# Gate products of a gated recurrence on half the rows, both gates in one product

## What is computed

```
xg = conv.reshape(B, T, LRU_BLOCKS, LRU_BLOCK_W)          # 8 blocks of 64 channels
r = sigmoid(einsum('btnd,nde->btne', xg, w_r) + b_r)
i = sigmoid(einsum('btnd,nde->btne', xg, w_i) + b_i)
log_a = -LRU_C * r * softplus(-lam);  a = exp(log_a)
mult = where(pos == 0, 1, sqrt(-expm1(2 * log_a)))
u = mult * i * conv
h_t = a_t * h_(t-1) + u_t
```

## Time and profile before

| | us |
|---|---|
| median of 3 runs (701.61 to 701.86) | 701.74 |
| the profiled execution | 701.76 |
| its span, first to last instruction | 700.0 |
| TensorE busy | 692.3 (99%), 4688 products |
| VectorE busy | 303.2 (43%) |
| ScalarE busy | 263.0 (38%), 642 instructions |
| POOL busy | 106.1 (15%) |

### The profile page before, as it was taken

How to read it: one execution, slowest core, us unless ns; L and a number is a source line. 1 busy time by engine, 2 the same in 40 slices (tenths; PEclk the granted TensorE clock), 3 DMA queues, 4 the chain that set the end, 5 groups by cost and what they waited for, 6 DMA issues and landing times.

```text
span 700.0 us, 11867 instructions
## 1 busy us (share of the span) xinstructions
PE 692.3 (99%) x4688; PEld 671.7 (96%) x4688; DVE 303.2 (43%) x668; ACT 263.0 (38%) x642; POOL 106.1 (15%) x231
## 2 busy tenths in 40 slices
PE   8999999999999999999999999999999999999998
PEld 8999998999999999999999999899999999999998
DVE  6462452343434448875433374317533672500000
ACT  7562242322323343756616555325543460200000
POOL 0002171435354000000002222122100000000000
DMA  8402105122120311011041010131001351522221
GB/s 301 183 0 92 61 1 194 48 65 61 51 75 7 119 61 60 7 56 61 1 145 66 11 61 1 49 97 62 1 1 61 119 183 32 166 71 64 65 66 37
DMA packets 26803, 50.07 MB, mean 72 GB/s; under 512 B 2232, under 2 KB 20152, under 8 KB 24540
## 3 DMA queue, kind: packets, MB, share of 16 engines
q1 hardware_dynamic: 26748, 49.31, 21.4%
HBM read 42.22 MB, written 9.12 MB: 73 GB/s over the span
## 4 chain that ended last, share of the span: by engine, by line
PE 96%; DMA 1%; DVE 1%; issue 1%; ACT 1%; POOL 0%; SPq 0%; DVEq 0%; ACTq 0%
PE proj L409 22%; PE proj L411 22%; PE proj L410 22%; PE branch L411 4%; PE branch L410 4%; PE branch L409 4%; PE branch L589 2%; PE branch L654 2%; PE branch L631 2%; PE branch L505 1%; PE branch L522 1%; PE branch L537 1%; PE branch L543 1%; PE branch L644 1%; PE branch L525 1%; DMA mixed<-x_T 1%
## 5 line engine op out<-in xcount | busy, mean ns | idle before, releaser
L409 PE MATMUL proj<-big 128*128 128x352 f32 (+1 forms) x952 | 305.8, 321 | 1.6 <-DVE big L1148 1.2
L411 PE MATMUL proj<-big 128*128 128x352 f32 (+1 forms) x952 | 290.8, 305 | 0.0
L410 PE MATMUL proj<-big 128*128 128x352 f32 (+1 forms) x952 | 290.8, 305 | 0.0
L409 PEld LDWEIGHTS proj<-big 128*128 128x128 f32 x952 | 179.3, 188 | 5.4 <-ACT big L814 2.0
L410 PEld LDWEIGHTS proj<-big 128*128 128x128 f32 x952 | 179.4, 188 | 2.6 <-issue 1.9
L411 PEld LDWEIGHTS proj<-big 128*128 128x128 f32 x952 | 179.3, 188 | 0.0
L1143 DVE TENSOR_TENSOR big<-raw,big 128x512 fp32r<-128x512 f32 x72 | 48.8, 689 | 39.3 <-ACT big L808 39.3
L1588 POOL TENSOR_SCALAR stat<-stat 128x1 f32<-128x1 f32 (+2 forms) x68 | 18.0, 264 | 278.7 <-ACT junk L934 189.5
L411 PE MATMUL branch<-m_hi,big 128*128 128x352 f32 x180 | 58.0, 322 | 0.0
L410 PE MATMUL branch<-m_lo,big 128*128 128x352 f32 x180 | 58.0, 322 | 0.0
L409 PE MATMUL branch<-m_hi,big 128*128 128x352 f32 x180 | 57.9, 322 | 0.0
(11 more groups left out here) (219 smaller groups left out, 964.5 us busy)
## 6 DMA issues: line engine op xcount, KB each, us to landing
raw<-w_units SPq DMA_DIRECT2D x17, 1024.0 KB, 4.9
mixed<-x_T SPq DMA_DIRECT2D x12, 352.0 KB, 7.9
xy<-x_T SPq DMA_DIRECT2D x24, 176.0 KB, 2.4
out_y_T<-xy SPq DMA_DIRECT2D x24, 176.0 KB, 1.9
raw<-w_out SPq DMA_DIRECT2D x6, 512.0 KB, 4.5
xy<-w_out SPq DMA_DIRECT2D x6, 512.0 KB, 4.2
s<-state_ret SPq DMA_DIRECT2D x4, 512.0 KB, 3.9
out_s_ret<-s SPq DMA_DIRECT2D x4, 512.0 KB, 3.2
```

Source lines behind the costliest of these rows:

```text
L409: pe.matmul(out, a_lo, b_hi, start=first, stop=False)
L410: pe.matmul(out, a_hi, b_lo, start=False, stop=False)
L411: return pe.matmul(out, a_hi, b_hi, start=False, stop=last)
```

## The change

The gate weights are laid out anew: for stage h, the upper 64 partitions hold the r and the i block of the first 64 channels side by side (64 x 128), the lower 64 partitions the i and the r block of the other 64 channels. A product uses 64 partitions of weights and input and gives both gates of 64 channels. There are still 6 per stage, now two for each chunk (upper, lower) in banks 0 to 4 and 0. Each bank is read by two tangents of 64 partitions, so 12 per stage; one of the two moves its half to the other 64 partitions (in the upper product the second, in the lower the first), so all count in `gates_read` is doubled. The sixth product waits for 12f+2. The first tangent of a stage now waits for `lru_set` f (from f = 1 on) besides the product. On ScalarE the stage is split over three slots: tangents of the first two chunks at the old slot, the last chunk one slot later, the decay step two slots later; the slots of m2, root and scan move by two. The biases are laid out to match.

```
-            wg = sb("wg", [P, 2, H, P], scope=r)
+            wg = sb("wg", [P, H, P], scope=r)
...
-            ("conv", (90, 98, 108, 119)), ("gates", (95, 106, 117, 128)), ("m2", (100, 111, 122, 133)),
-            ("sqrt", (101, 112, 123, 134)), ("scan", (102, 113, 124, 135)))}
+            ("conv", (90, 98, 108, 119)), ("gates", (95, 106, 117, 128)), ("last", (96, 107, 118, 129)),
+            ("decay", (97, 108, 119, 130)), ("m2", (102, 113, 124, 135)), ("sqrt", (103, 114, 125, 136)),
+            ("scan", (104, 115, 126, 137)))}
...
-            GATE_BANKS = [0, 1, 2, 3, 4, 0]
...
-                for q in range(6):
-                    gate, c = divmod(q, 3)
-                    if q == 5:
-                        pe.wait_ge(S_["gates_read"], 6 * f + 1)
-                    elif f > 0:
-                        pe.wait_ge(S_["gates_read"], 6 * f)
-                    pe.matmul(bb[GATE_BANKS[q]][:, 0:CH], wg[:, gate, f, :], cv[:, f % 2, c * CH:(c + 1) * CH],
-                              start=True, stop=True).then_inc(S_["gates_done"], 1)
+                for c in range(3):
+                    for part in range(2):
+                        q, rows = 2 * c + part, slice(64 * part, 64 * part + 64)
+                        if q == 5:
+                            pe.wait_ge(S_["gates_read"], 12 * f + 2)
+                        elif f > 0:
+                            pe.wait_ge(S_["gates_read"], 12 * f)
+                        pe.matmul(bb[q % 5][:, 0:CH], wg[rows, f, :], cv[rows, f % 2, c * CH:(c + 1) * CH],
+                                  start=True, stop=True).then_inc(S_["gates_done"], 1)
...
-            def lru_sig(f):
...
+            def lru_sig(f, cs):
+                if f >= 1:
+                    act.wait_ge(S_["lru_set"], f)
+                if f == 0:
+                    act.wait_ge(S_["decay_set"], 1)
+                low, high = slice(0, 64), slice(64, P)
+                for c in cs:
+                    cols = slice(c * CH, (c + 1) * CH)
+                    for part in range(2):
+
+                        q = 2 * c + part
+                        act.wait_ge(S_["gates_done"], 6 * f + q + 1)
+                        bank, b = bb[q % 5], half_b[:, H * part + f:H * part + f + 1]
+                        first = rgs[low, f % 2, cols] if part == 0 else ig[high, cols]
+                        second = ig[low, cols] if part == 0 else rgs[high, f % 2, cols]
+                        act.activation(first, bank[low, 0:CH], ACT.Tanh, bias=b[low], scale=0.5).then_inc(
+                            S_["gates_read"], 1)
+                        act.activation(second, bank[high, 0:CH], ACT.Tanh, bias=b[high], scale=0.5).then_inc(
+                            S_["gates_read"], 1)
+
+            def lru_decay(f):
+                act.wait_ge(S_["gates_read"], 12 * f + 12)
...
                 if (u, s) in LRU_AT["gates"]:
-                    lru_sig(LRU_AT["gates"][u, s])
+                    lru_sig(LRU_AT["gates"][u, s], (0, 1))
+                if (u, s) in LRU_AT["last"]:
+                    lru_sig(LRU_AT["last"][u, s], (2,))
+                if (u, s) in LRU_AT["decay"]:
+                    lru_decay(LRU_AT["decay"][u, s])
...
-    wg = np.zeros((P, 2, H, P), np.float32)
...
+    wg = np.zeros((P, H, P), np.float32)
+    r_blocks, i_blocks = f["w_rgate"][0], f["w_igate"][0]
+    for h in range(H):
+        wg[:64, h] = np.concatenate([r_blocks[2 * h], i_blocks[2 * h]], axis=1)
+        wg[64:, h] = np.concatenate([i_blocks[2 * h + 1], r_blocks[2 * h + 1]], axis=1)
```

More of the change, by code:

```diff
@@ L316, in _ @@
             sp.wait_ge(S_["stored_ret"], 32 * H)
-            sp.dma_start(wg[:].rearrange("p a h n -> p (a h n)"), io["w_gates"]).then_inc(S_["wg_in"], 16)
+            sp.dma_start(wg[:].rearrange("p h n -> p (h n)"), io["w_gates"]).then_inc(S_["wg_in"], 16)
             for u in range(9, 13):
@@ L582, in lru_gates @@
                     pe.wait_ge(S_["mix_a"], 36)
[L583 to L590 removed]
+                for c in range(3):
[7 more added lines that the diff above has]
+                                  start=True, stop=True).then_inc(S_["gates_done"], 1)
             def turn_tails():
                 pe.wait_ge(S_["lru_set"], H)
[L594 removed]
+                pe.wait_ge(S_["gates_read"], 48)
                 for f in range(H):
@@ L608, in turn_k @@
                 else:
-                    pe.wait_ge(S_["gates_read"], 24)
+                    pe.wait_ge(S_["gates_read"], 48)
                 pe.transpose(bb[0][:, 0:n], kn[0:n, n9 % 2, :], ident[0:n, 0:n]).then_inc(S_["kT_done"], 1)
@@ L892, in ret_norm @@
                     act.activation(o_nrm[:, m % 2, 0:NS], bb[1 + m % 2][:, 0:NS], ACT.Copy).then_inc(S_["o_set"], 1)
-            def lru_sig(f):
[L895 to L906, removed]
-                                   ACT.Tanh, bias=half_b[:, col:col + 1], scale=0.5).then_inc(S_["gates_read"], 1)
-                act.wait_ge(S_["gates_read"], 6 * f + 6)
+            def lru_sig(f, cs):
[18 more added lines that the diff above has]
+                act.wait_ge(S_["gates_read"], 12 * f + 12)
                 if f > 0:
@@ L1720, in laid_out @@
     put("conv_b", f["conv_b"].reshape(H, P))
-    put("b_r", f["b_rgate"].reshape(H, P))
-    put("b_i", f["b_igate"].reshape(H, P))
+    b_r, b_i = f["b_rgate"].reshape(H, P), f["b_igate"].reshape(H, P)
+    put("b_r", np.concatenate([b_r[:, :64], b_i[:, :64]], axis=1))
+    put("b_i", np.concatenate([b_i[:, 64:], b_r[:, 64:]], axis=1))
     put("lam", f["lru_lambda"].reshape(H, P))
@@ L1728, in laid_out @@
             par[r, PAR["sink_s"] + half] = f["attn_sinks"][0, 2 * half + r // DS % 2]
-    wg = np.zeros((P, 2, H, P), np.float32)
-    for a, name in enumerate(("w_rgate", "w_igate")):
-        blocks = f[name][0]
-        for n in range(2 * H):
-            r = slice(64 * (n % 2), 64 * (n % 2) + 64)
-            wg[r, a, n // 2, r] = blocks[n]
+    wg = np.zeros((P, H, P), np.float32)
[3 more added lines that the diff above has]
+        wg[64:, h] = np.concatenate([i_blocks[2 * h + 1], r_blocks[2 * h + 1]], axis=1)
     x = np.concatenate([f["x_prompt"].reshape(SEQ, D), f["x_sample"].reshape(NS, D)])
@@ L1741, in laid_out @@
         "qk_gain": np.concatenate([f["q_norm_g"][0], f["k_norm_g"][0]]),
-        "w_gates": wg.reshape(P, 2 * H * P), "state_ret": f["state_ret"][0],
+        "w_gates": wg.reshape(P, H * P), "state_ret": f["state_ret"][0],
         "cache_k": f["cache_swa_k"][0],
```

## The result

The changed kernel took 711.93 us (median of 4 runs, 711.7 to 712.61) against 701.67 us before (4 runs, 701.4 to 701.86): ratio 1.0143, interval 1.0131 to 1.0156. It is 10 us slower, clear of the noise, where I had forecast 1 us, and outside my range. The profiled execution took 711.70 us, its span is 709.9, 9.9 more than before.

What follows compares the result with a forecast made beforehand. TensorE's queue was taken as the bound (busy 692.3 of 700.0 us). Stages 0 to 3 gave -1.3 + 0 + 0 + 2.0, changes of shape 0.3: +1.0 on 701.76, 702.8 us; range 699.8 to 704.9.

Steps and rivals of the forecast that it cites:

- Stage 0: First gate stage: overlapping products save 1.48 us, the sixth product is 0.2 us late; -1.3 us.
- seven steps: Gate products of a stage: 7 overlapped steps of 0.296 us instead of 12, 2.07 us against 3.55.
- 0 to 0.9 us for four stages: TensorE entering and leaving the 64-row shape: 0 to 0.11 us each way; 0.3 us taken in all.
- The half tangent: ScalarE's 64-partition tangents: each costs a whole one, 0.553 us, starting 0.445 us after the one before.
- Stage 1: Second gate stage: TensorE idles 1.2 us behind table load and tangents, cancelling the overlap; scan just in time; 0.0 us.
- Stage 2: Third gate stage: TensorE idles 1.2 us behind table load and tangents, cancelling the overlap; scan has 1 us of room; 0.0 us.
- Rival (c): Table loads of stages 1 and 2 run ahead and scans come sooner, saving 1.3 us each; 700.2 us, chance 0.09.
- Stage 3: Last gate stage: root behind two Silu rows delays scan and tangents, TensorE idles 3.2 us; +2.0 us.
- rival (b): TensorE drops to half clock after the stall of stage 3, costing 2.6 us; 705.4 us, chance 0.10.
- the 1.25 us here did no such harm: Longest idle time named in the profile before: next passes started 0.16 us apart, so no slower clock followed.
- rival (a): Upper and lower half products do not overlap, so stage 0 gains nothing; +2.3 us, 704.1 us, chance 0.20.

Runs made afterwards that it cites:

- the schedule alone: Kernel before, with its 128-row products and whole tangents, given the slots, waits and three-part ScalarE work of the change; 704.41 us, ratio 1.0035.
- old root slots: Changed kernel with only m2, root and scan put back in the slots of before; 705.67 us, ratio 1.0044.
- one half only: Changed kernel with all six products on the upper 64 rows of weights and input; 708.54 us, ratio 1.0083.
- order of the half tangents: Changed kernel, first product in a free projection bank, only stage 0's m2, root, scan in changed slots; each chunk's tangents read lower rows first; 700.5 us.
- the pair with the same holds: Kernel before with 6, 6, 4, 6 extra ScalarE copies holding the sixth product: 712.74 us with full rows, 721.91 with products cut to upper 64 rows.

## Why the prediction was wrong, point by point

**Stage 0**: the overlap was right, its form and the sizes not. Forecast -1.3 us, measured -0.6. The prediction let the second pass of a product run with the first pass of the next, seven steps; in the trace the first passes of an upper and a lower product run together, then their second passes, six steps. But the first step takes 0.40 us, and so does that of the sixth product, which stands alone behind a wait; that is no second change of shape, since the sixth product of 128 rows in stage 3 of the schedule alone, behind its 2.06 us, shows 0.40 us too. My 0 to 0.9 us for four stages with 0.3 taken was far too low: 0.39 us for each unbroken block. The sixth product started at 2.13 instead of 1.79: the first tangent came 0.17 us later than reckoned from the stage's first pass, the second 0.13 later (0.575 instead of 0.445 us), and the signal of 0.04 was left out.

**The half tangent.** "The partitions hardly count, a half costs a whole" was right for its duration, 0.55 us, and wrong for the distance: 0.575 us instead of 0.445. I had taken a distance from full tangents for a shape that has none in the trace of before. ScalarE's busy time rose by 14.7 us, forecast 13.

**Stage 1**: "The two meet: no further stall, and no room" was the step that failed first, and the change's own idle time grew by it. The scan of stage 0 started at 275.48, not 274.1, and its last product released the first tangent at 281.23. VectorE had waited for the second weight copy, which stands behind all twelve half tangents on ScalarE: 12 x 0.13 = 1.6 us late by the same distance. The convolution so began at 263.86 instead of 262.5. The prediction saw that stage 1 had no room and yet put it at 0.0, and idle time came to 2.17 us instead of 1.2.

**Stage 2** went as reckoned but for 0.3 us: load straight behind the first product, first tangent straight behind the load, idle time 1.37 us. Rival (c) is out: all three loads came behind the first product.

**Stage 3** is the best part of the forecast. Sixth product at 5.16 us forecast, 5.22 measured, with idle time 3.2 forecast and 3.18 measured. The chain Silu, load, root, scan that I had added up from single rows was right, and the kernel with the old root slots shows that it was the slot. Of the 3.5 us that the stage cost beyond the forecast 3.0 are the half clock; the other 0.5 us are not split up.

**The clock** was the largest miss, 6.4 of the 9.9 us. It was rival (b), with 0.10, one fall and 2.6 us, in stage 3 only. It came three times. The step at fault is where I let "the 1.25 us here did no such harm" speak for the stalls of 1.2 us in stages 1 and 2: that row has full-row products behind it, it is one idle time, and the stalls came out longer. The schedule alone, with full rows, bore 2.1 us and lost nothing; the change, with its 64 rows, fell after 1.37. The Trainium skill (TensorE: Matmul & The Clock Gate, "Why this matters for your kernels") warns against idle gaps between bursts, and I cited it as speaking for the long stall only; the trace agrees for that one, 3.18 us, and shows the fall behind 2.17 and 1.37 us as well.

**The forecast's sum** had the right sign and mechanism for all of the idle time in stage 3, and the overlap, which I took from the Trainium skill's page named in the prediction while no row of before showed it, is there: rival (a) is out. What the range lacked was the case in which (b) holds at every stall, 3 x 1.7 to 3.0 us.

## What to carry to other kernels

Putting two half-row products side by side in the array gives back half of their time less some 0.4 us a block, so keep a block unbroken: a bank that must be read in mid-block costs its wait, a slow first pass behind it and perhaps the clock. Price an idle time on TensorE twice, with what it lasts and with a stretch at half clock that may follow, here the more likely where the products around it used 64 rows. Look at the granted clock of every run and not of the profiled one alone. When the order of an engine's queue is changed by hand, follow each copy and evacuation that now stands behind the slower work, since here one weight copy set the stall of the next stage.

## What the runs showed of the hardware

- Two products on the upper and lower 64 rows start in the same 0.01 us and a pair of passes costs one, 0.296 us. The Trainium skill (TensorE: Matmul & The Clock Gate, "The mechanism") draws such starts a few ns apart; the trace agrees. The Trainium skill (TensorEngine Tiling (Array Packing), "Key Properties") also says that a change of mode drains TensorE; here that came to 0.39 us for going in and out.
- The first pass of the lower product starts ahead of the second pass of the upper one: from the first pass on, the passes of a stage start at 0, 0.01, 0.40 and 0.41 us.
- The order need not alternate: with three upper products ahead of three lower ones the tenth pass still started only 1.70 us behind the first, against 1.59.
- A tangent on 64 partitions lasts 0.55 us as on 128, but the next starts 0.575 us behind it, not 0.445: halves ran one after another with no overlap. Whether the same holds for other functions or other partition counts was not tried.
- Granted clock after an idle time between gate products, in the profiled runs: with 64 rows it fell after 1.37 (twice), 1.70, 2.0 (four times), 2.08, 2.15, 2.17, 3.07 and 3.18 us, not after 0.2 or 1.26 us. With full rows it fell after one of five idle times of 2.0 to 2.2 us and after all three of 2.9 and more, not after 1.56. In the first microseconds it fell behind 1.8 and 1.9 us of idle time with full rows as well (old root slots, one half only), when TensorE had only just begun.
- None of these lengths is a limit. By the mean granted clock of its single runs, the same kernel fell in one run and not in another: with idle times of 2.0 us (one half only), of 1.4 and 1.7 us (old root slots) and of 2.3 us (order of the half tangents). How long the record then shows 0.5, 3.4 or 6.8 us, does not follow from the idle time alone either: four holds of about equal length on half rows had both. What decides stays open. What is shown is the pair with the same holds, half clock in 20 to 25 us of each run with half rows and in 1 to 7 us of each with full rows.
